# Router, even attention and PEER stream starts: other products, another order, other engines

## The reference

```python
# MoE router
grp_logits = h @ w_grp + b_grp            # 4 groups
grp = argmax(grp_logits)
exp_logits = h @ w_exp + b_exp            # 32 experts, 8 in each group
top 2 of softmax(exp_logits of the group) -> experts and gates
# even mixer: 8 heads of sparse attention (DSA), 4 of differential attention
li = relu(q_idx . k_idx);  iscore = sum over heads of li * w_idx   # then causal
sel = top_k(iscore, 64)                   # a query attends to these keys only
o_a = softmax(q k + bias over sel) v
a = softmax(q1 k1 + bias) - lam * softmax(q2 k2 + bias);  o_b = a v
o_b = rmsnorm(o_b over the 128 columns of a head) * subln_g * (1 - lam_init)
y = concat(o_a, o_b) @ w_out;  x = x + g1 * y
# PEER: 8 heads, 16 experts each, out of 128 x 128 of one neuron each
q = h @ w_q;  s = q . sub_keys            # two halves, 128 keys each
top 16 of each half, top 16 of their sums -> experts, gates = softmax
out = sum over 128 picks of gates * gelu(h . u[e]) * v[e]
x = x + g2 * out
```

## Time and profile before

| | us |
|---|---|
| three runs | 2463.46, 2468.83, 2466.47 |
| median | 2466.47 |
| profiled execution | 2466.98 |
| its span in the trace | 2465.2 |

### The profile page before, as it was taken

The page is one execution under the profiler, slowest core; times in us unless marked ns, Lnnn a source line. Parts: engine busy times, 40 slices in busy tenths (PEclk is TensorE's granted clock), DMA queues, the critical chain, the costliest instruction groups (busy, mean ns, idle before and its releaser), DMA issues. The chain is left out here.

```text
span 2465.2 us, 24127 instructions
## 1 busy us (share of the span) xinstructions
PE 1921.0 (78%) x8926; PEld 1027.6 (42%) x8926; DVE 1358.2 (55%) x3249; ACT 324.2 (13%) x799; POOL 556.9 (23%) x563
## 2 busy tenths in 40 slices
PE   6998666666579689877777877788899877777776
PEld 4666333333266365432322322374565333223222
DVE  2623000001167647768877786555287787777865
ACT  1052000000111421000000000113311100000000
POOL 1000000000000013334444444100035444344432
PEclk9998878888889799999999999998999999999999
DMA  9987999999798049999999999693299999999996
GB/s 381 409 256 299 428 428 430 429 430 428 297 353 327 35 168 374 420 418 421 420 419 419 422 403 421 282 374 137 71 357 422 421 421 420 417 414 420 421 421 286
DMA packets 145522, 894.76 MB, mean 363 GB/s; under 512 B 17304, under 2 KB 29432, under 8 KB 62456
## 3 DMA queue, kind: packets, MB, share of 16 engines
q0 software_dynamic: 73728, 536.90, 52.8%
q1 hardware_dynamic: 71672, 356.25, 36.3%
HBM read 889.68 MB, written 3.42 MB: 362 GB/s over the span
## 5 line engine op out<-in xcount | busy, mean ns | idle before, releaser
L1471 PE MATMUL psum<-sb_area 128*128 128x512 f32 x2048 | 975.4, 620 | 270.8 <-DVE sb_area L2028 267.8
L696 POOL DMA_INDIRECT sb_area<-in_peer_uv,sb_peer_e x512 | 546.2, 1067 | 1106.2 <-PE psum L1471 730.0
L2042 DVE CUSTOM_DVE_ANT_0 sb_area<-sb_area 128x1024 f32<-128x1024 f32 x512 | 626.6, 1224 | 285.4 <-DMA sb_area<-in_peer_uv,sb_peer_e 283.1
L1471 PEld LDWEIGHTS psum<-sb_area 128*128 128x128 f32 x2048 | 383.9, 195 | 819.5 <-DVE sb_area L2028 433.8
L1193 PE MATMUL psum<-sb_area 128*32 128x256 f32 x2048 | 172.4, 511 | 136.3 <-DMA sb_area<-in_moe_w_gu 134.4
L1670 DVE COPY sb_area<-psum 128x128 f32<-128x128 f32 x32 | 9.3, 292 | 397.8 <-PE psum L1203 397.8
L965 ACT ACTIVATE sb_small<-sb_small 128x2 f32<-128x2 f32 x256 | 52.1, 204 | 1187.0 <-DVE sb_small L2042 1187.0
L1009 PE MATMUL psum<-sb_area 128*128 128x256 f32 x912 | 203.5, 385 | 5.1 <-ACT sb_area L740 3.5
L2028 DVE SCALAR_TENSOR_TENSOR sb_area<-sb_ident,sb_small,sb_area 128x128 f32<-128x128 f32 x512 | 156.1, 346 | 60.8 <-ACT sb_small L965 56.1
L1009 PEld LDWEIGHTS psum<-sb_area 128*128 128x128 f32 x912 | 175.1, 193 | 34.8 <-issue 5.1
L1193 PEld LDWEIGHTS psum<-sb_area 128*32 128x32 f32 x2048 | 82.7, 146 | 225.8 <-DMA sb_area<-in_moe_w_gu 147.8
(11 more groups left out here) (282 smaller groups left out, 1385.2 us busy)
## 6 DMA issues: line engine op xcount, KB each, us to landing
sb_area<-in_moe_w_gu SPq DMA_DIRECT2D x32, 4096.0 KB, 33.5
sb_area<-in_ada_w SPq DMA_DIRECT2D x72, 1024.0 KB, 12.9
sb_area<-in_moe_w_dn SPq DMA_DIRECT2D x32, 2048.0 KB, 24.1
sb_area<-in_peer_w_q SPq DMA_DIRECT2D x8, 2048.0 KB, 7.9
sb_area<-in_sb_w_in SPq DMA_DIRECT2D x6, 2048.0 KB, 21.7
sb_area<-in_odd_w_in SPq DMA_DIRECT2D x6, 2048.0 KB, 13.2
sb_area<-in_even_w_in SPq DMA_DIRECT2D x5, 2048.0 KB, 17.9
sb_area<-in_peer_uv,sb_peer_e POOLq DMA_INDIRECT x512, 13.0
```

The costliest lines, as they stand in the source:

```text
L696: pool.indirect_dma_start(uv_rows[s], None, rows, bass.IndirectOffsetOnAxis(ap=peer_e[:, m:m + 1], axis=0)).then_inc(named(f"uv_loaded{s}" ...
L1471: last = pe.matmul(ps[:, 4 + 2 * t + half, :], diag[:, s, :], uv_rows[s][:, D + half * HALF:D + (half + 1) * HALF], start=(k == 0), stop=( ...
L2042: dve.tensor_tensor_reduce(uv_rows[s][:, 0:D], uv_rows[s][:, 0:D], h_tok[:, m // P, :], 1.0, 0.0, ALU.mult, ALU.add, dots[:, m % BODY:m % ...
```

## The change

**Router.** The weights are now the stationary operand: eight products give the logits transposed, 36 x 256. VectorE adds the bias as a column, and two transposes bring them to tokens. Four of the sixteen transposes of `hT` stand between. **After the MoE** the dummy product is gone, and VectorE waits for the last combination, behind its branch, itself. **Even mixer**: w_idx is loaded and projected with group W (the former T); the steps of the adaLN thirds come one head later; the mask is added to the maps by GpSimd, a pair of maps at a time. The diff heads go first. Their squares, sums (onto 32 partitions each), variance, root and reciprocal are on 256 columns, and four products with a broadcast column of the identity spread the result back. **PEER**: an `ACT.Gelu` on a dummy column follows the first gate exponentials; the gate row is made at pick 90 and taken at 94, on another bank; groups 2 and 3 have one product a pick over 32 picks; the tables of picks are new.

```diff
-SEARCH_AT = 4
-EXP_AT = 22
-PROJECT_AT = {2: 0, 3: 26}
-TAKE_AT = {2: 20, 3: 46}
-KEYS_AT = {2: 24, 3: 50}
-COPY_AT = {2: 32, 3: 58}
+SEARCH_AT = 8
+EXP_AT = 26
+PROJECT_AT = {2: 2, 3: 36}
+TAKE_AT = {2: 36, 3: 68}
+KEYS_AT = {2: 37, 3: 69}
+COPY_AT = {2: 40, 3: 72}
+ROW_AT = 90
+ROW_TAKE_AT = 94
...
-            group("even", w[:, 512:a], "T", hT, ckv_tok)
+            group("even", w[:, 512:a], "W", hT, ckv_tok, beside=w[:, kk:b])
             group("even", w[:, a:i], "F", hT, qidx)
-            group("even", w[:, i:b], "I", hT, None)
+            group("even", w[:, i:kk], "I", hT, None)
...
+        PAIR_ORDER = {"even": [4, 5, 6, 7, 0, 1, 2, 3], "odd": list(range(PAIRS_OF))}
...
+                elif g["kind"] == "W":
+                    sp.dma_start(slot[:, 0:nk, 0:cols], w).then_inc(w_loaded[n % 3], 16)
+                    sp.dma_start(slot[:, 0:nk, cols:cols + IDX_HEADS], g["beside"].rearrange("(k p) n -> p k n", p=P),
+                                 allow_slow_non_contiguous=True).then_inc(w_loaded[n % 3], 16)
...
-            load_mixer("even", BY_STAGE["even"][0], [0, 0, 6, 6, 3, 4, 4, 1, 0, 0, 0], begun=2)
+            load_mixer("even", BY_STAGE["even"][0], [0, 0, 3, 5, 6, 4, 4, 2, 0, 0, 0], begun=2)
...
+            pool.wait_ge(named("rel_loaded"), 32)
+            pool.wait_ge(named("idx_masked"), 1)
+            for p in range(DSA_HEADS // 2):
+                maps = rel_maps[:, 2 * p:2 * p + 2, :]
+                pool.tensor_tensor(maps, maps, idx_mask.unsqueeze(1).broadcast_to([P, 2, MAPW]), ALU.add
+                                   ).then_inc(named("maps_masked"), 1)
...
+                    if stage == "even" and i == PAIRS_OF - 1:
+                        act.wait_ge(named("pair_weighed"), DIFF_HEADS)
+                        act.activation(diff_sq.rearrange("p h t -> p (h t)"), ps[:, 2:4, :].rearrange("p b n -> p (b n)"),
+                                       ACT.Square).then_inc(named("diff_sq_done"), 1)
+                        act.wait_ge(named("subln_made"), 1)
+                        act.activation(oT[:, 4:8, :].rearrange("p h t -> p (h t)"), ps[:, 2:4, :].rearrange("p b n -> p (b n)"),
+                                       ACT.Copy, scale=subln_col[:, 0:1]).then_inc(named("diff_scaled"), 1)
+                    if stage == "even" and i == PAIRS_OF + 1:
+                        act.wait_ge(named("diff_var_done"), 1)
+                        act.activation(diff_std, diff_std, ACT.Sqrt).then_inc(named("diff_std_done"), 1)
+                    if i >= 3 and not is_diff(stage, order[i - 3]):
...
                 exp_gates(0)
+                act.activation(warm[:, :], ones[:, 0:1], ACT.Gelu_apprx_tanh)
                 take(*groups_here[1])
-                take_row(stage, 4)
...
+                    if (b + 1) * BATCH == ROW_TAKE_AT:
+                        take_row(stage, 6)
...
+            for k in range(KC):
+                last = pe.matmul(ps[0:ROUTES, 4, 0:T], route_w[:, k, :], hT[:, k, :], start=(k == 0), stop=(k == KC - 1))
+            last.then_inc(named("logits_summed"), 1)
+            turn_tokens(0)
+            pe.wait_ge(named("logits_biased"), 1)
+            for t in range(NT):
+                last = pe.transpose(ps[:, 4, t * 64:t * 64 + ROUTES], logits_T[0:ROUTES, t * P:(t + 1) * P], ident[0:ROUTES, 0:ROUTES])
+            last.then_inc(named("logits_done"), 1)
+            for b in range(1, 4):
+                turn_tokens(b)
             make_row("moe", 6)
...
-            pe.matmul(ps[0:1, 4, 0:1], zeros[:, 0:1], ones[:, 0:1], start=True, stop=True).then_inc(named("moe_combined"), 1)
...
+                    if stage == "even" and i == PAIRS_OF:
+                        pe.wait_ge(named("diff_sq_done"), 1)
+                        for h in range(DIFF_HEADS):
+                            last = pe.matmul(ps[32 * h:32 * (h + 1), 7, 0:T], ones[:, 0:32], diff_sq[:, h, :], start=True, stop=True,
+                                             skip_group_check=True)
+                        last.then_inc(named("diff_summed"), 1)
...
-            sum_third(4)
             pe.wait_ge(proj_out, even[2][0] + 1)
             for i in range(4):
                 idx_scores(2 * i)
                 idx_scores(2 * i + 1)
                 project(*even[3 + i])
                 if i in (0, 2):
+                    sum_third(4 + i // 2)
+                if i in (1, 3):
                     turn_row(4 + i // 2)
-                if i in (1, 3):
-                    sum_third(5 + i // 2)
             pe.wait_ge(named("ckvT_ready"), 1)
             project(*even[7])
+            sum_third(6)
             project(*even[8])
             turn_row(6)
...
             make_row("even", 0)
-            pe.wait_ge(named("diff_sq_done"), 1)
-            for half in range(2):
-                last = pe.matmul(ps[:, 4 + half, :], ones[:, :], diff_sq[:, 2 * half:2 * half + 2, :].rearrange("p h t -> p (h t)"),
-                                 start=True, stop=True)
-            last.then_inc(named("diff_summed"), 1)
+            pe.wait_ge(named("diff_inv_made"), 1)
+            pe.wait_ge(named("diff_scaled"), 1)
+            for h in range(DIFF_HEADS):
+                last = pe.matmul(ps[:, 2 + h // 2, h % 2 * T:(h % 2 + 1) * T], ident[:, 32 * h:32 * h + 1].broadcast_to([P, P]),
+                                 diff_std, start=True, stop=True, skip_group_check=True)
+            last.then_inc(named("diff_spread"), 1)
...
-                    for q in (2 * at, 2 * at + 1):
-                        f, k = q // KC, q % KC
-                        last = pe.matmul(ps[:, b + f // 2, (f % 2) * T:(f % 2 + 1) * T], wring[n % 3][:, k, f * P:(f + 1) * P],
-                                         hT[:, k, :], start=(k == 0), stop=(k == KC - 1), skip_group_check=True)
-                    if at == 2 * KC - 1:
+                    f, k = at // KC, at % KC
+                    last = pe.matmul(ps[:, b + f // 2, (f % 2) * T:(f % 2 + 1) * T], wring[n % 3][:, k, f * P:(f + 1) * P],
+                                     hT[:, k, :], start=(k == 0), stop=(k == KC - 1), skip_group_check=True)
+                    if at == 4 * KC - 1:
...
-                make_row(stage, 4)
...
+                        if PROJECT_AT[i] <= m < PROJECT_AT[i] + 4 * KC:
...
+                    if m == ROW_AT:
+                        pe.wait_ge(named("keys_copied"), KEY_PARTS * (L + 1))
+                        make_row(stage, 6)
                     if m == P:
-                        pe.wait_ge(named("keys_copied"), KEY_PARTS * (L + 1))
+                        pe.wait_ge(row_loaded, 16 * ROW_TURN[stage])
                     weigh(m)
...
+                dve.wait_ge(named("comb_done"), p * EXPERTS + EXPERTS)
+                dve.memset(most[:, 7:8], 0.0)
...
+                dve.wait_ge(named("route_loaded"), 64)
+                dve.wait_ge(named("logits_summed"), 1)
+                dve.tensor_scalar(logits_T[0:ROUTES, :], ps[0:ROUTES, 4, 0:T], route_b[0:ROUTES, 0:1], None, ALU.add
+                                  ).then_inc(named("logits_biased"), 1)
...
-            dve.wait_ge(named("moe_combined"), 1)
+            dve.wait_ge(named("comb_done"), EXPERTS)
...
+                    if stage == "even" and i == PAIRS_OF:
+                        dve.wait_ge(named("diff_summed"), 1)
+                        dve.tensor_scalar(diff_std, ps[:, 7, 0:T], 0.5 / HEAD, EPS, ALU.mult, ALU.add).then_inc(named("diff_var_done"), 1)
...
+                    if stage == "even" and DIFF_HEADS - 1 <= i < PAIRS_OF - 1:
+                        dve.wait_ge(named("maps_masked"), i - DIFF_HEADS + 2)
...
-            copy_row(4)
...
                 if h in (3, 7):
-                    take_third(4 + h // 7)
+                    copy_row(4 + h // 7)
                 if h == 5:
-                    copy_row(5)
+                    take_third(4)
...
+                if r == DSA_TOP // 16:
+                    take_third(5)
                 for t in range(NT):
                     step(dve.max(idx_top, both_tiles(idx_score, t)))
                     step(dve.match_replace(both_tiles(idx_score, t), idx_top, both_tiles(idx_score, t), TAKEN))
-            step(dve.tensor_scalar(idx_mask, idx_score, TAKEN, NEG, ALU.not_equal, ALU.mult))
+            dve.tensor_scalar(idx_mask, idx_score, TAKEN, NEG, ALU.not_equal, ALU.mult).then_inc(named("idx_masked"), 1)
+            dve.wait_ge(named("rel_loaded"), 32)
             copy_row(6)
-            dve.wait_ge(named("rel_loaded"), 32)
-            dsa_maps = rel_maps[:, 0:DSA_HEADS, :]
-            step(dve.tensor_tensor(dsa_maps, dsa_maps, idx_mask.unsqueeze(1).broadcast_to([P, DSA_HEADS, MAPW]), ALU.add))
             take_third(6)
...
-            dve.wait_ge(named("diff_summed"), 1)
-            dve.tensor_scalar(diff_std.rearrange("p h t -> p (h t)"), ps[:, 4:6, :].rearrange("p b n -> p (b n)"), 0.5 / HEAD, EPS,
-                              ALU.mult, ALU.add).then_inc(named("diff_var_done"), 1)
```

(8 more changed lines are left out.)

101 lines of the change are left out of this document (44 added, 57 removed).

## The result

The changed kernel takes 2443.85 us in the median of four runs (2442.03 to 2445.61), the kernel before 2464.97 (four runs, 2462.27 to 2468.83): 21.1 us less, a ratio of 0.991 with a 95% interval of 0.9894 to 0.9926. The prediction was 2445.6, a gain of 20.9. The profiled executions are 2466.98 and 2443.41 with spans of 2465.2 and 2441.7, so 23.5 lie between the two traces.

A forecast was written before the change was run, and what follows sets the result against it. Expert-row streams were taken as DMA-bound, leaving edits only DMA idle time behind late compute. Gains of 4.1 + 3.4 + 1.4 + 4.0 + 4.5 + 3.5 = 20.9 us gave 2445.6, range 2438 to 2457.

The forecast's parts named there:

- Router: Logits by eight wide products, not 36 narrow instructions, shorten TensorE's chain before the expert choice: 4.1 us, range 3.4 to 4.3.
- Seam: After the MoE, VectorE waits for the last real product instead of a dummy: 3.4 us, range 2 to 3.6.
- Projections: Even mixer's projections: DMA-bound stretch with the same bytes ahead of the last adaLN piece, so 0 gain.
- Mask: Even mixer: mask addition moves to GpSimd, hidden, so scoring waits only for scores: 1.4 us, range 1.2 to 1.7.
- Tail: Last exponential to output projection in the even attention falls from 19.7 to 15.7 us: 4.0, range 0 to 6.
- Stream starts: Starts of both expert-row streams: earlier table load and one product a pick save 4.5 us in peer0, 3.5 in peer1.
- TensorE, not DMA, is the bound in 32 picks: Stream starts: a pick with projection takes TensorE 2.58 us against 2.51 for its gather; one product makes it 2.15.
- (A): Rival: thinner picks let TensorE's clock fall to 1.2 GHz while projecting, making the kernel slower, up to 2495 us; 3%.
- (B): Rival: stream starts give the table load alone, VectorE's search or gather latency setting the pace: 2451.0 us; 15%.
- (C): Rival: GpSimd's mask additions and VectorE's normings stall one another in the first diff pairs: about 2450.6 us; 10%.
- (D): Rival: stream starts lose nothing any more, or the table load's own idle stretch goes too: 2442.8 us; 12%.
- (E): Rival: the attention's tail gets no shorter because the new waits chain up: 2449.6 us; 10%.

The follow-up runs named there:

- b_peer: The kernel before with only the PEER half of the changed kernel: 2456.72 us against 2465.37, ratio 0.9965.
- a_nodummy: The changed kernel without the dummy gelu, so the first gelu loads the table again: 2452.01 us in one run.
- b_warmroute: The kernel before with dummy products on TensorE in its two idle stretches ahead of the router: 2460.75 us against 2464.82, ratio 0.9980.

## Why the prediction was right, point by point

The mechanisms of the router, the seam, the mask and the tail are the right ones, and these four are 12.9 of the 20.9. That the total came within 0.2 us of the forecast is luck: its interval is 18 to 26, the stages by themselves add up to 24.0, one gain of 1.6 was not in the sum, and the 8.0 of the stream starts had a wrong reason for their larger part.

- **Router, 4.1 forecast, 4.7 measured.** The counts were right; the durations of transposes and row were taken from rows at a clock of 0.50, and behind the new products they ran at 1.00 each time. That gave 0.8 more up to the choice in the mean (1.4 against the profile of before), and a little is lost again in the first expert's products. The mean lies above the stated range of 3.4 to 4.3.
- **Seam, 3.4 and 3.3.** Right in each step: ScalarE took over as the last one, as the text had it.
- **Projections, 0.** The stretch from the first square of fin1 to the diagonal mask is 109.8 after and 110.0 before. Right.
- **Mask, 1.4 and 1.6.** GpSimd's 1.78 an addition lies between the two bounds of 0.84 and 2.5.
- **Tail, 4.0 and 5.5.** The chain came as written, 15.3 us in the mean and 14.4 in the changed kernel's profile against 15.7, with the new waits it names, and 1.0 more came ahead of the last exponential. The range of 0 to 6 holds it. TensorE's clock moves the tail as the range allowed for: in the changed kernel's profile it is 0.61 in the mean from 823 to 827 and 1.00 from 828 to 837.
- **Missed: the output projection, 1.6.** I had ended the sum at its start. TensorE had idled 10 us ahead of it and paid for that afterwards too.
- **Stream starts, 8.0 forecast, 7.3 by the stages and 8.65 by b_peer.** The size was right, the step "TensorE, not DMA, is the bound in 32 picks" was wrong as the main cause: two products a pick cost 0 to 1.2 us a stream, and the figures of that step, 2.58 and 2.51, give 2.2 at most. What counted was how early the first reissue comes, and the places in the tables. The late start was worth 2.3 and 1.8, not 1.3. In peer1 the first gelu came 20.04 us behind the first gather and now comes after 18.22: 1.28 is the load, and the other 0.5 is the gate row, whose taking stood ahead of it on ScalarE (1.03 at 1809.87). The clock has no part in that 1.8; it is at 1.00 there in all five old profiles. In peer0 it adds 0.4 to the mean, by the two profiles in which it fell. The 349 GB/s that bounded peer0's gain at 6.6 was one of these two.
- **Rivals.** (A) had the clock fall in the thinner picks; it stays at 1.00 in the first 40 us. (B) is out by b_peer. (C) has no sign, but no norming ran beside an addition, see above. (D), nothing lost any more or an idle stretch with the table load: a load in the wrong place does cost 3.0 (a_nodummy), 1.28 by itself and 1.6 through TensorE's clock. In a_nodummy the gelu starts at 1798.70, 0.01 behind the load's end. The drain that the Trainium skill adds to each switch ("ScalarE: Activation LUTs", section "What ACT_TABLE_LOAD costs") is not seen on ScalarE there. (E) is out.

## What to carry to other kernels

Where several engines hand work to each other, cost TensorE's idle time twice: once as a wait and once in what it runs next. Idle stretches of 3 to 10 us went with blocks of instructions up to 1.7 times as long here (transposes 3.42 and 1.96), and filling some with dummy products, with one square root moved, was worth half of this whole change again. To find what a soft start of a DMA-bound stream costs, cut the rates into short windows and undo one cause at a time: the first window belonged to the late reissue and the next to the schedule. And compare stages over several profiles: the odd mixer, which the change doesn't touch, moved by 7 us between profiles, a third of the whole gain.

## What the hardware showed beyond that

- Eight products of 36 columns (sixteen instructions) take 3.63 us at a granted clock of 0.50 and 1.98 at 1.00, and eight of 256 columns 3.64 at 1.00. While narrow products ran, the clock fell from 1.00 to 0.50 (b_warmroute, 197 to 201 us); behind the products of 256 columns the transposes ran on at 1.00 (changed kernel, 201 to 203).
- Behind 10.31 us of idle time TensorE had a mean clock of 0.62 over the first four microseconds, behind 1.31 us 1.00. Behind 2.85 us eight instructions took 5.34 us (clock 0.50 from 1800 to 1802), behind 1.43 us 3.70. Behind 1.99 us in peer1 of before the clock stayed at 1.00.
- An addition of 128x768 with two SBUF operands takes 1.78 us on GpSimd; VectorE does four of them in one instruction in 3.35.
